# Making the block inverses of a two-direction scan once for two steps, by halves and in place

## The chip, the core and the metric

The kernel runs on one NeuronCore of a Trainium2 chip, in float32 throughout. The metric is the device time of one execution in microseconds (us). Of three runs of the kernel before, the median is 1346.3 us (1344.57 to 1348.67).

## The reference, cut to what matters

One layer of a hybrid diffusion backbone over 1024 latent tokens and 256 context tokens, width 1024: modulation, a combined input projection with a short convolution, a token mixer, an output projection, and a mixture of 16 experts. The change lies in the token mixer, which has a gated DeltaNet group (4 heads of 128) and a Mamba-2 SSD group (8 heads of 64), each run in both directions, context first:

```
decay = exp(G[i] - G[j]) for i >= j              # G: cumulated log gates of a chunk
L     = strict_lower((beta k) k^T * decay)
u, w  = solve(L + I, [beta v, beta k exp(G)])     # unit triangular
v_new = u - w S
o     = (q exp(G)) S + (q k^T * decay) v_new
S     = S exp(g_last) + k_tail^T v_new

# SSD group, per chunk
y_off  = C h * exp(a)
y_diag = (C B^T * exp(a[i] - a[j])) (x * dt)
h      = h exp(a_last) + B^T (x * dt * exp(a_last - a))
```

## The kernel before

The sequence is cut into ten chunks of 128 tokens (two of context, eight of latents). The scan is a list of twenty steps, `steps[s] = (s % 2, s // 2)`: direction d = 0 and d = 1 take turns, so that an even step is a chunk of the forward direction and the odd one after it a chunk of the backward direction. Steps 0 to 3 are context (only states), steps 4 to 19 are latent (states and outputs). No planner orders the work: each engine has its own loop over `s`, written out by hand, and semaphores tie the loops together. Within an iteration `s` an engine does things for `own` (step s), `nxt` (s + 1), `two` (s + 2) and `three` (s + 3).

TensorE (`pe_scan`), in the order of one iteration: `from_k` (key by state, L429), `block_w(nxt)`, `from_state` (L511), `solve` (L429), `block_vy(nxt)`, `from_chunk` (L522), `outputs` (L495, L496), `block_vp(nxt)`, `to_s` (L429), `to_state` (L532), `block_vq(nxt)`. Every float32 matmul here is two instructions in the trace. L448 is the one line of the four `block_` functions.

The triangular inverse of a 128-token chunk is made from the inverses of its four 32 x 32 diagonal blocks, which an earlier stage has left in DRAM (`xy_dram`) as X and as its transpose Y. `block_w` multiplies the off-diagonal part AT (key products times decays) by the diagonal inverses, and three more products (`vy`, `vp`, `vq`) put the blocks together. Between them ScalarE copies the products W and Q out of PSUM (`evac`, L601), and VectorE makes Y of them (`block_p`, L658, and `block_y`, L664). All of it is done for the next step during this one, with matmuls of 64 to 128 columns.

VectorE also masks the decays that a DMA has broadcast (`mask_dn`, 512 wide, and `mask_ssm`, 1024 wide, both L633), multiplies AT by them (`block_a`, L653), and does `rest` (L669), `scores` (L715), `y_off` (L699), `y_diag` (L706), `new_s` (L679) and `new_hs` (L691). ScalarE takes exponentials in place (`decay`, L565, `decay8`, L577), scales the keys (`tail_k`, L595) and the SSD input by the step size (`scaled_x`, L586), and copies U and the outputs. GpSimd does `query_e` (L770), `with_eg` (L754, L756), `decayed_hs` (L764) and `tail_x` (L777).

SyncE (SP) issues every load and store of the scan from one queue, in the order of `sp_scan`: for each step s three transfers of key products (`load_at(two)`, L834), four of the diagonal inverses (`load_xy(two)`, L844; both X and Y, written into one buffer for each direction), then `load_kg(two)` (L851), `load_e(three)` (L822), `load_e8(two)` (L859), `load_qk(two)` (L866), `load_kt(two)` (L872), and last `scan_store(own)` (L918), which waits until the outputs of this step are complete:

```
sp_.wait_ge(sem("s_o"), turn(d, nl(step) + 1))
sp_.wait_ge(sem("s_yd"), turn(d, nl(step) + 1))
```

`load_e8(two)` waits for `from_chunk` of this step, since that frees the buffer.

Ahead of the scan, `gates_second` on ScalarE (L2108 to L2110) takes three exponentials of gate columns, for which VectorE waits before `wtail` (L2363).

Of the kernel before, what the change touches and what calls it, by code (L numbers as in the profile page):

```python
# [5 lines left out]
P = 128  # L6
F32 = mybir.dt.float32
U32 = mybir.dt.uint32
ALU = mybir.AluOpType
# [6 lines left out]
def hybrid_block(nc, x, c, ctx, c_ctx, ada_w, ada_b, norm_g, w_in, conv_w, conv_b, dn_A_log, dn_dt_bias,  # L16
# [47 lines left out]
    with ExitStack() as es:  # L64
# [37 lines left out]
        eps1, eps_q = sb("eps1", [P, 1]), sb("eps_q", [P, 1])  # L102
# [213 lines left out]
        E, AT, Xd, Yd, W, Y, Q, kgT, qgT, QE, ktail, R, U, S = ([] for _ in range(14))  # L316
        E8, xdt, xw, hs, ost, XY = ([] for _ in range(6))
        for d in range(2):
            for lst in (W, Y, Q, kgT, qgT):
                lst.append(take(L4).rearrange("p (h n) -> p h n", h=DN_H))  # L320
            if d == 1:
# [6 lines left out]
                for dd in range(2):  # L328
                    XY.append(take(2 * L4).rearrange("p (x n) -> p x n", n=P))
                    Xd.append(XY[dd][:, 0:DN_H, :])  # L330
                    Yd.append(XY[dd][:, DN_H:2 * DN_H, :])
            for lst in (QE, ktail, R, U, S):
                lst.append(take(L4).rearrange("p (h n) -> p h n", h=DN_H))
            E8.append(take(SSM_H * P).rearrange("p (h n) -> p h n", h=SSM_H))
            for lst in (xdt, xw, hs):
# [14 lines left out]
        HI, TOP = slice(P // 2, P), slice(0, P - BL)  # L350
        A_R = ((TOP, slice(BL, P)), (slice(0, P), TOP))
        W_R = ((slice(0, P), slice(0, P)), (TOP, slice(BL, P)))
        Q_R = ((TOP, HI), (TOP, slice(0, P // 2)))
        Y_R = ((slice(0, P // 2), HI), (HI, slice(0, P // 2)))
# [54 lines left out]

        def hold(bank, n):  # L410
# [5 lines left out]
        def pe_first(pe):  # L416
            pe.wait_ge(sem("pfree"), NM - 1)
            pe.wait_ge(sem("s_at"), 1)
            pe.wait_ge(sem("ld_xy0"), 64)
            for h in range(DN_H):  # L420
                last = nc.tensor.matmul(bA[0][:, cols(h)], AT[0][:, h, :], Xd[0][:, h, :], start=True, stop=True)
            last.then_inc(sem("s_blk"), 1)

        def pe_scan(pe):
# [19 lines left out]
            def in_region(d, rc, lhsT, rhs, k=slice(0, P)):  # L444

                rows, cc = rc
                for h in range(DN_H):
                    last = mm(heads(bA[d][:])[rows, h, cc], lhsT[k, h, rows], rhs[k, h, cc], start=True, stop=True)  # L448
                return last

            def block_w(step):
                d, n = step
                pe.wait_ge(sem("s_at"), turn(d, n + 1))
                pe.wait_ge(sem(f"ld_xy{d}"), 64 * (n + 1))
                if n > 0:
                    pe.wait_ge(sem("s_py"), part(2, (d, n - 1), 2))
                in_region(d, W_R[d], AT[d], Xd[d]).then_inc(sem("s_blk"), 1)

            def block_vy(step):
                d, n = step  # L460
# [2060 lines left out]
```

## Time and profile before

| | |
|---|---|
| median of three runs | 1346.3 us (1344.57 to 1348.67) |
| the profiled execution: its time | 1342.35 us |
| its span, first to last instruction | 1340.6 us |
| TensorE busy | 1228.4 us, 92% |
| VectorE, ScalarE, GpSimd busy | 768.7, 429.4, 226.2 us |
| the scan | from about 550 us to about 756 us of the span |

The span is cut by the profiler into instructions with a start and a busy time. Matmuls are pipelined: the busy time of a group ends later than the next group begins, so the cost of a group on TensorE is read from its start to the start of the next one. An idle time in square brackets stands behind the instruction that ended it, with what released it.

### The profile page before, as it was taken

The numbers are of one execution on the slowest core, as the hardware profiler recorded it, in microseconds if no ns is written. First come the engines' busy times: TensorE is split into PE (matmuls) and PEld (weight loads), VectorE is DVE, ScalarE is ACT, GpSimd is POOL, SyncE is SP. The second block draws the span as 40 slices with busy tenths as digits, with TensorE's granted clock in tenths as the row PEclk, the third lists the DMA queues.
The fourth block names the chain that finished last, engine by engine and source line by source line (L and its number), as shares of the span: only waits on it lengthen the run. The fifth ranks groups of instructions, "written<-read, shape, count | busy, mean of one in ns | idle before, by whom it ended". The sixth has DMA issues, their size and how long they took to land.

```text
span 1340.6 us, 14739 instructions
## 1 busy us (share of the span) xinstructions
PE 1228.4 (92%) x5500; PEld 711.8 (53%) x5500; DVE 768.7 (57%) x1113; ACT 429.4 (32%) x1109; POOL 226.2 (17%) x205
## 2 busy tenths in 40 slices
PE   4999999999998999899999989981799999999992
PEld 3555555555544555588999744440444444444440
DVE  5299889887926778579898656647300101010116
ACT  5333232313111112567887545531101011010123
POOL 0300000020000021165677100001100101010112
PEclk9999999999998999999999999995799999999996
DMA  9923455442142443376766755526599999999967
GB/s 366 287 79 102 124 162 150 142 146 94 48 128 77 90 94 85 80 205 199 223 211 207 265 203 188 188 79 227 199 346 339 332 341 324 349 320 353 319 221 184
DMA packets 206164, 270.69 MB, mean 202 GB/s; under 512 B 73685, under 2 KB 122830, under 8 KB 206094
## 3 DMA queue, kind: packets, MB, share of 16 engines
q1 hardware_dynamic: 186182, 212.54, 48.2%
q0 software_dynamic: 13840, 50.86, 12.4%
q10 hardware_dynamic: 6072, 6.35, 1.4%
q8 instruction: 44, 0.72, 0.2%
q14 instruction: 26, 0.21, 0.1%
HBM read 217.75 MB, written 51.97 MB: 201 GB/s over the span
## 4 chain that ended last, share of the span: by engine, by line
PE 73%; DVE 13%; DMA 8%; SPq 2%; ACT 2%; issue 1%; POOLq 0%; DVEq 0%; ACTq 0%
PE ps L2045 18%; PE ps L1210 17%; PE ps L1233 8%; PE ps L1165 7%; PE ps L448 4%; PE ps L429 4%; DVE arena L2412 3%; DMA tok_dram<-arena 2%; DVE arena L2483 2%; DVE arena L2481 2%; DMA arena<-w_in 2%; DMA arena<-ada_w 1%; PE ps L522 1%; PE ps L1944 1%; PE ps L495 1%
## 5 line engine op out<-in xcount | busy, mean ns | idle before, releaser
L2045 PE MATMUL ps<-arena 128*128 128x512 f32 (+1 forms) x1072 | 424.9, 554 | 5.3 <-DMA arena<-w_in 5.3
L2045 PEld LDWEIGHTS ps<-arena 128*128 128x128 f32 x1072 | 201.6, 191 | 205.9 <-issue 195.4
L1210 PE MATMUL ps<-arena 128*128 128x512 f32 x512 | 226.8, 596 | 1.4 <-ACT arena L1359 1.4
L2412 DVE SCALAR_TENSOR_TENSOR arena<-arena,taps 128x1024 f32<-128x1024 f32 x160 | 207.5, 1297 | 5.5
L1210 PEld LDWEIGHTS ps<-arena 128*128 128x128 f32 x512 | 96.5, 191 | 116.6 <-issue 114.8
L1560 DVE TENSOR_TENSOR arena<-arena,ps 128x512 f32<-128x512 f32 x16 | 11.0, 688 | 223.3 <-PE ps L1210 223.3
L1165 PE MATMUL ps<-arena 128*128 128x512 f32 x256 | 115.5, 597 | 2.9 <-DMA arena<-w_out 2.9
L1233 PE MATMUL ps<-arena 128*128 128x512 f32 x256 | 112.5, 592 | 0.0
L448 PE MATMUL ps<-arena 128*128 128x128 f32 (+5 forms) x632 | 69.6, 253 | 7.6 <-DVE arena L658 3.9
L1233 PEld LDWEIGHTS ps<-arena 128*128 128x128 f32 x256 | 47.5, 190 | 54.0 <-issue 54.0
L1165 PEld LDWEIGHTS ps<-arena 128*128 128x128 f32 x256 | 46.5, 190 | 53.4 <-issue 49.5
L1377 ACT ACTIVATE arena<-ps 128x512 f32<-128x512 f32 x16 | 9.6, 598 | 198.7 <-PE ps L1210 198.7
L1642 POOL DMA_INDIRECT y_dram<-arena x14 | 22.3, 1594 | 289.5 <-DVE arena L1567 289.5
L448 PEld LDWEIGHTS ps<-arena 128*128 128x128 f32 (+4 forms) x632 | 62.4, 168 | 15.3 <-issue 8.7
L2227 ACT ACTIVATE arena<-arena,vcols 128x1280 f32<-128x1280 f32 (+1 forms) x20 | 25.9, 1297 | 137.0 <-DVE arena L2412 136.8
L1359 ACT ACTIVATE arena<-ps 128x512 f32<-128x512 f32 x32 | 19.0, 594 | 143.4 <-PE ps L1199 143.4
L1566 DVE TENSOR_SCALAR arena<-ps,arena 128x512 f32<-128x512 f32 x14 | 10.5, 750 | 91.7 <-PE ps L1233 91.7
L429 PE MATMUL ps<-arena 128*128 128x128 f32 x448 | 62.4, 282 | 0.2 <-DVE arena L669 0.2
L2428 DVE SCALAR_TENSOR_TENSOR arena<-arena,silu_c 128x256 f32<-128x256 f32 x112 | 57.0, 509 | 4.0
L1850 POOL DMA_DIRECT2D arena<-ada_w x16 | 14.4, 902 | 259.3 <-DVE arena L2428 217.9
L429 PEld LDWEIGHTS ps<-arena 128*128 128x128 f32 x448 | 55.3, 191 | 3.5 <-issue 1.5
L633 DVE TENSOR_TENSOR arena<-arena,neg_mask 128x512 f32<-128x512 f32 (+1 forms) x36 | 47.4, 1318 | 2.8 <-DMA arena<-g_dram 2.7
(336 smaller groups left out, 1579.2 us busy)
## 6 DMA issues: line engine op xcount, KB each, us to landing
arena<-exp_w_gate SPq DMA_DIRECT2D x16, 2048.0 KB, 11.1
arena<-exp_w_up SPq DMA_DIRECT2D x16, 2048.0 KB, 9.5
arena<-exp_w_down SPq DMA_DIRECT2D x16, 2048.0 KB, 10.8
arena<-ada_w POOLq DMA_DIRECT2D x16, 1024.0 KB, 6.4
arena<-w_in SPq DMA_DIRECT2D x28, 512.0 KB, 4.8
arena<-ada_w SPq DMA_DIRECT2D x4, 2048.0 KB, 19.6
arena<-x SPq DMA_DIRECT2D x16, 512.0 KB, 6.4
arena<-g_dram SPq DMA_DIRECT2D x16, 512.0 KB, 5.7
```

What stands on the lines that cost most here:

```text
L429: last = mm(out[:, h * P:(h + 1) * P], lhsT[:, h, :], rhs[:, h, :], start=True, stop=True)
L448: last = mm(heads(bA[d][:])[rows, h, cc], lhsT[k, h, rows], rhs[k, h, cc], start=True, stop=True)
L633: return nc.vector.tensor_tensor(out, out, bh(neg_mask[:, d, :], n), ALU.add)
L1165: last = mm(ps[2 + 2 * s + h][:], mixT[s][:, k, :], wo[:, k, h * 512:(h + 1) * 512], start=(k == 0), stop=(k == KD - 1))
L1210: last = mm(ps[gu_bank[s] + j][:], xsT[s][:, k, :], ew[s][j][:, k, :], start=(k == 0), stop=(k == KD - 1))
L1233: last = mm(ps[down_bank(e) + h][:], hidT[s][:, k, :], ew[s][2][:, k, h * 512:(h + 1) * 512], start=(k == 0), stop=(k == KF - 1))
L2045: last = mm(ps[3 * (m % 2) + gi][:, 0:w], wring[(m + 1) % NW][:, k, :], hT[:, k, o:o + w], start=(k == 0), stop=(k == KD - 1))
L2227: ins = a(dst, cacc[n_conv(mm) % 2][:, 0:w], ACT.Silu, bias=bcol)
L2412: ins = v.scalar_tensor_tensor(accg, cin_l[ci % 2][:, j // 3:j // 3 + GR, j % 3:j % 3 + GW], tp[:, j:j + 1], accg, ALU.mult, ALU.add)
L2428: ins = v.scalar_tensor_tensor(out, blk[:, k, :], silu_c[:, k, 0:1], out, ALU.mult, ALU.add)
L2481: link(v.tensor_tensor(tm, yo4[:, :, j, j + 1:BL].unsqueeze(3).to_broadcast([P, 3, n, j]), z4[:, :, j, 0:j].unsqueeze(2).to_broadcast([P, ...
L2483: link(v.tensor_tensor(z4[:, :, j + 1:BL, 0:j], z4[:, :, j + 1:BL, 0:j], tm, ALU.subtract))
```

## The change

- **Blocks for two steps at once, by halves.** In odd iterations only, the inverses of both directions of the next pair n are made: `block_near` (32 x 32 products of neighbouring blocks), `block_pairs`, `block_far` (64 x 64), `block_halves`. ScalarE takes all four out of PSUM (`near_out`, `pairs_out`, `far_out`, `halves_out`) and writes the results, negated, straight into the X and Y that the DMA has brought. W, Q, the four older block functions, `block_p` and `block_y` are gone. For a pair there are 16, then 16 and 8, then 8, then 8 matmuls.
- **Loads.** `load_at` for steps s + 2 and s + 3 and `load_xy` for the same two are issued together in even iterations; d = 1 gets two XY buffers in turn. `load_at` waits for `block_far` of the pair before.
- **Decays one step further ahead.** `load_e` and `mask_dn` are for s + 4, `decay` for s + 3.
- **Step size in the exponent.** A logarithm of the step size is added to the bias of `decay8`, so `scaled_x` falls away and `from_chunk` takes x itself.
- **Order.** `from_chunk` comes behind `outputs` and `to_s`; `mask_ssm(nxt)` comes ahead of `scores(own)`; `y_diag` comes behind `new_s`.

```diff
+        PAIRS = (((0, 1), (2, 3)), ((1, 0), (3, 2)))
+        FROM, INTO = (half(0), half(1)), (half(1), half(0))
...
+        def near(n, ds):
+            for h in range(DN_H):
+                for k in range(2):
+                    for d in ds:
+                        a, b = PAIRS[d][k]
+                        last = nc.tensor.matmul(heads(bA[d][:])[quarter(b), h, 0:BL], AT[d][quarter(a), h, quarter(b)],
+                                                x_of(d, n)[quarter(a), h, quarter(a)], start=True, stop=True)
+            return last
...
+            def block_near(n):
+                pe.wait_ge(sem("s_at"), turn(1, n + 1))
+                for d in range(2):
+                    pe.wait_ge(sem(f"ld_xy{d}"), 64 * (n + 1))
+                near(n, (0, 1) if n > 0 else (1,)).then_inc(sem("s_blk"), 1)
...
+            def block_far(n):
+                pe.wait_ge(sem("s_wq"), phase(n, 2))
+                for h in range(DN_H):
+                    for d in range(2):
+                        last = mm(heads(bA[d][:])[INTO[d], h, HALF:P], AT[d][FROM[d], h, INTO[d]],
+                                  x_of(d, n)[FROM[d], h, FROM[d]], start=True, stop=True)
+                last.then_inc(sem("s_blk"), 1)
...
             for s in range(-1, 2 * NS):
                 own = steps[s] if s >= 0 else None
-                nxt = steps[s + 1] if s + 1 < 2 * NS else None
+                n = pair_of(s)
                 if own and own[1] > 0:
                     from_k(own)
-                if own and nxt:
-                    block_w(nxt)
+                if n is not None:
+                    block_near(n)
                 if lat(own):
                     from_state(own)
                 if own:
                     solve(own)
-                if nxt:
-                    block_vy(nxt)
+                if n is not None:
+                    block_pairs(n)
+                if lat(own):
+                    outputs(own)
+                if own and own[1] < LAST:
+                    to_s(own)
+                if n is not None:
+                    block_far(n)
                 if lat(own):
                     from_chunk(own)
-                    outputs(own)
-                if nxt:
-                    block_vp(nxt)
                 if own and own[1] < LAST:
-                    to_s(own)
                     to_state(own)
-                if nxt:
-                    block_vq(nxt)
+                if n is not None:
+                    block_halves(n)
...
+            def pairs_out(n):
+                act.wait_ge(sem("s_blk"), phase(n, 2))
+                for d in range(2):
+                    a_, b = PAIRS[d][d]
+                    minus(x_of(d, n)[quarter(b), :, quarter(a_)], heads(bA[d][:])[quarter(b), :, BL:2 * BL])
+                    for a_, b in PAIRS[d]:
+                        last = minus(y_of(d, n)[quarter(a_), :, quarter(b)], heads(bA[d][:])[quarter(a_), :, 0:BL])
+                last.then_inc(sem("s_wq"), 1)
...
                 if own and own[1] > 0:
                     rest(own)
-                if lat(own):
-                    scores(own)
-                if own and two:
-                    mask_dn(dve, two)
-                if lat(own):
-                    y_off(own)
-                if nxt:
-                    block_p(nxt)
                 if lat(nxt):
                     mask_ssm(nxt)
                 if lat(own):
-                    y_diag(own)
-                if two:
+                    scores(own)
+                    y_off(own)
+                if s % 2 == 0 and two:
                     block_a(two)
+                    block_a(three)
+                if four:
+                    mask_dn(dve, four)
                 if own and own[1] < LAST:
                     new_s(own)
+                if lat(own):
+                    y_diag(own)
+                if own and own[1] < LAST:
                     new_hs(own)
-                if nxt:
-                    block_y(nxt)
...
-                    sp_.wait_ge(sem("s_blk"), part(4, (d, n - 1), 1))
+                    sp_.wait_ge(sem("s_blk"), phase(n - 1, 3))
...
-                if two:
+                four = steps[s + 4] if s + 4 < 2 * NS else None
+                if s % 2 == 0 and two:
                     load_at(two)
-                    load_xy(two)
+                    load_at(three)
+                if four:
+                    load_e(four)
                 if two and two[1] > 0:
                     load_kg(two)
-                if three:
-                    load_e(three)
+                if s % 2 == 0 and two:
+                    load_xy(three)
+                    load_xy(two)
                 if lat(two):
                     load_e8(two)
                     load_qk(two)
...
                 a(eGt[:], gb[:], ACT.Exp).then_inc(sem("g_act"), 1)
+                act.wait_ge(sem("g_act"), 6)
+                a(gb[:], sp[:], ACT.Ln, bias=tiny[:])
                 a(wtail[:], ga[:], ACT.Exp).then_inc(sem("g_act"), 1)
```

## Rows read from the trace of the kernel before

**Rows 1.** Busy time of each engine in one stretch of the latent steps, with granted clock

```profile
core 0: us, PE busy (x) PEld busy (x) DVE busy (x) ACT busy (x) POOL busy (x), PEclk, DMA share, GB/s
661.00:682.00 21.00, 21.00 (x224) 19.52 (x223) 18.73 (x29) 15.09 (x49) 15.33 (x11) 1.00 0.71 223
```

**Rows 2.** Timeline of TensorE, one even step: start us, busy us, instructions

```profile
665.91 1.06 PE L448 MATMUL ps<-arena 128*128 128x128 f32 x8
666.80 1.03 PE L511 MATMUL ps<-arena 128*128 128x256 f32 x4
...
668.56 1.06 PE L448 MATMUL ps<-arena 128*128 128x128 f32 x8
669.55 1.15 PE L522 MATMUL ps<-arena 128*64 128x64 f32 x32
670.63 0.49 PE L495 MATMUL ps<-arena 128*128 128x128 f32 x2
...
672.52 0.81 PE L448 MATMUL ps<-arena 128*96 128x64 f32 x8
673.17 1.11 PE L429 MATMUL ps<-arena 128*128 128x128 f32 x8
...
675.07 0.68 PE L448 MATMUL ps<-arena 96*64 96x64 f32 x8
675.68 1.16 PE L429 MATMUL ps<-arena 128*128 128x128 f32 x8
676.68 0.84 PE L448 MATMUL ps<-arena 128*96 128x96 f32 x8
```

**Rows 3.** Timeline of the DMA-issuing queue of SyncE in the scan

```profile
655.32 0.32 SPq L918 DMA_DIRECT2D scan_dram<-arena  x1
655.68 2.62 SPq L834 DMA_DIRECT2D arena<-kk_dram  x3
658.34 2.08 SPq L844 DMA_DIRECT2D arena<-xy_dram  x4
660.47 0.45 SPq L851 DMA_DIRECT2D arena<-eg_dram  x1
...
661.44 0.42 SPq L859 DMA_DIRECT2D arena<-g_dram  x1
...
679.16 3.36 SPq L844 DMA_DIRECT2D arena<-xy_dram  x4
```

**Rows 4.** Line L834: one issue, all 60 (ns min/median/max)

```profile
L834 SPq DMA_DIRECT2D arena<-kk_dram x60: 550/599/1597, 522.5 to 731.7; - x60
```

**Rows 5.** Line L844, issue to landing

```profile
DMA to landing us min/median/max: 1.7/2.0/4.0
```

**Rows 6.** Line L859, issue to landing

```profile
DMA to landing us min/median/max: 3.9/5.7/6.8
```

**Rows 7.** Groups by line and shape, 640 to 740 us

```profile
L577 ACT ACTIVATE arena<-arena,ga 128x128 f32<-128x128 f32 x80 | 24.3, 389 | 0.0
L633 DVE TENSOR_TENSOR arena<-arena,neg_mask 128x1024 f32<-128x1024 f32 x9 | 14.9, 1651 | 0.0
L715 DVE TENSOR_TENSOR arena<-arena 128x512 f32<-128x512 f32 x18 | 12.6, 743 | 0.0
L601 ACT ACTIVATE arena<-ps 96x256 f32<-96x256 f32 x10 | 3.7, 374 | 5.4 <-PE ps L448 5.4
```

**Rows 8.** Timeline of TensorE: start of the scan, steps 2, 4 and 18, end

```profile
553.38 1.13 PE L448 MATMUL ps<-arena 128*128 128x128 f32 x8 [1.93 <-ACT arena L601]
...
574.15 1.13 PE L429 MATMUL ps<-arena 128*128 128x128 f32 x8 [0.19 <-DVE arena L669]
...
591.01 1.13 PE L429 MATMUL ps<-arena 128*128 128x128 f32 x8
...
742.34 1.05 PE L429 MATMUL ps<-arena 128*128 128x128 f32 x8
...
755.61 0.39 PE L496 MATMUL ps<-arena 128*128 128x128 f32 x2
```

**Rows 9.** Timeline of ScalarE and VectorE around the gates

```profile
103.66 1.28 ACT L2227 ACT_TABLE_LOAD   x1
...
120.78 1.36 ACT L2227 ACTIVATE arena<-arena,vcols 128x1280 f32<-128x1280 f32 x1 [5.96 <-DVE arena L2412]
...
103.67 0.33 DVE L2363 TENSOR_TENSOR wtail<-wtail,sp 128x160 f32<-128x160 f32 x1 [1.05 <-ACT wtail L2110]
```

More of the change, by code:

```diff
@@ L408, in d_reader, with pair_of @@
             return {"yoff": "s_yoff", "ydiag": "s_yd"}[use2], turn(d, n - NC + 1)
+        def pair_of(s):
+            n = (s + 1) // 2
+            return n if s % 2 == 1 and n < NS else None
         def hold(bank, n):
@@ L627, in act_scan @@
                     a(ost[d][:, 0:QK], bC[d][:], ACT.Copy).then_inc(sem("s_o"), 1)
-                if nxt and nxt[1] < LAST:
+                if nxt and nxt[1] < LAST and s >= 0:
                     tail_k(nxt)
+                if n is not None:
+                    far_out(n)
+                    if lat(nxt):
+                        decay8(nxt)
+                    halves_out(n)
+                if s == -1:
+                    tail_k(nxt)
+                    decay(act, three)
         def masked(out, d, n):
@@ L721, in dve_scan @@
                 two = steps[s + 2] if s + 2 < 2 * NS else None
+                three = steps[s + 3] if s + 3 < 2 * NS else None
+                four = steps[s + 4] if s + 4 < 2 * NS else None
                 if own and own[1] > 0:
                     rest(own)
-                if lat(own):
-                    scores(own)
-                if own and two:
-                    mask_dn(dve, two)
-                if lat(own):
-                    y_off(own)
-                if nxt:
-                    block_p(nxt)
                 if lat(nxt):
@@ L887, in sp_scan @@
             sp_.wait_ge(sem("w_used"), NM + 1)
+            for step in steps[0:2]:
+                load_kt(step)
             sp_.wait_ge(sem("aux_used"), N_AUX)
             sp_.wait_ge(sem("ztok_out"), 16 * DI // P)
-            for s in range(-2, 2 * NS):
-                own = steps[s] if s >= 0 else None
+            for step in steps[2:4]:
+                load_e(step)
+            for s in range(0, 2 * NS):
+                own = steps[s]
                 two = steps[s + 2] if s + 2 < 2 * NS else None
                 three = steps[s + 3] if s + 3 < 2 * NS else None
-                if s < 0:
-                    load_kt(two)
-                    if s == -1:
-                        load_e(three)
-                    continue
-                if two:
+                four = steps[s + 4] if s + 4 < 2 * NS else None
+                if s % 2 == 0 and two:
                     load_at(two)
-                    load_xy(two)
+                    load_at(three)
+                if four:
+                    load_e(four)
                 if two and two[1] > 0:
                     load_kg(two)
-                if three:
-                    load_e(three)
+                if s % 2 == 0 and two:
+                    load_xy(three)
+                    load_xy(two)
                 if lat(two):
```

185 lines of the change are left out of this document (97 added, 88 removed).

## The prediction

> **What bounds the kernel now.** I first read the busy time by stretches. In the latent steps TensorE is busy 21.00 of 21.00 us at a granted clock of 1.00 (2.4 GHz), VectorE 18.73, ScalarE 15.09 [rows 1]. So the scan is bound by TensorE's own work, and what the change takes off TensorE counts, as far as nothing else is then late. Next the timeline of TensorE, for the price of each piece, from start to start [rows 2]. An even step lasts 676.68 - 665.91 = 10.77 us. Of it the block work (L448) is 0.89 + 0.99 + 0.65 + 0.61 = 3.14 us; in the odd step the first piece is narrower (busy 0.84 where the wide one shows 1.06), so about 0.67 and 2.92 in all. A pair of steps holds 6.06 us of block work. Of the rest I take from the same rows: `from_state` and `solve` 0.88 each (1.76 together), `from_chunk` 1.08, `outputs` 1.89, `to_s` and `to_state` 0.95 each, `from_k` 1.00: 7.63 a step. Third, the SyncE queue [rows 3, 4], since it issues every load in one order. Last, four times at which the scan stands: `solve` of step 2 at 574.15, of step 4 at 591.01, of step 18 at 742.34, the end at about 755.8 [rows 8]. Steps 4 to 18 are seven pairs in 151.3 us, 21.6 us a pair.
>
> **TensorE work, less.** A pair now has 56 small matmuls, two instructions each: 32 (near) + 48 (pairs) + 16 (far) + 16 (halves) = 112. No row shows 32 x 32 matmuls with four places of the array taking turns. The nearest is `from_chunk`: 32 instructions of 64 x 64 whose halves alternate, in 1.08 us, 0.034 us each. Upper bound: the 64-column block product, whose matmuls all go to one place, 8 in 0.61 us, 0.076 each [rows 2]. Lower bound: half the narrowest price, 0.017, as the matmuls have half the columns. I take 0.034: near 1.1, pairs 1.6, far 0.55, halves 0.55, 3.8 us, and 0.4 for more changes of shape (the first `outputs` group is busy 0.49 behind such a change [rows 2], which I read as 0.1 each). So TensorE has 4.2 us where it had 6.06, 1.9 less a pair; bound by TensorE alone a pair is 2 x 7.63 + 4.2 = 19.5 us.
>
> The row gives 0.034 us for an instruction. The Trainium skill ("TensorE: Matmul & The Clock Gate", Wait — 56ns, not 53.3ns?) has starts of matmuls never closer than about 25 ns, however small; by that estimate the 112 would be 2.8 us and not 3.8, and no lower than that.
>
> **ScalarE and VectorE, less.** `scaled_x` (eight copies) is gone. The new copies: twelve of 32 to 128 partitions. A 256-column one is 0.374 busy [rows 7]; back to back I take 0.28, and 0.18 for 128 columns: `near_out` 0.45, `pairs_out` (six) 1.2, `far_out` 0.65, `halves_out` 0.65, some 3 us a pair. Both engines have room [rows 1]. `block_p` and `block_y` leave VectorE. These gains are off the path.
>
> **SyncE: the loads come in one lump.** Here the gain goes. In an even iteration the queue issues two `load_at`, `load_e`, `load_kg`, two `load_xy`, and only then `load_e8`. Prices: three AT issues 3 x 0.6 plus gaps, 1.9 to 2.66, I take 2.05; four XY 2.13, at times 3.4 [rows 3, 4]; kg and e together 0.97 (660.47 to 661.44). Sum: 4.1 + 1.0 + 4.25 = 9.35 us, and 0.7 for an occasional long issue as at 679.16. The lump begins only when `scan_store` of the odd step before has been issued, which waits for `y_diag`. Call that moment 0. The last XY issue ends at 10.05 and lands 2.0 after its start [rows 5]: 11.5. `block_near` waits for both directions' XY, and behind it on TensorE stand `from_state`, `solve`, `outputs`, everything of the odd step. Without that wait TensorE would be there at about 9.7: `y_diag`, the store and its waits leave it some 1.2 us ahead, and the even step is 7.63 plus `to_state`, `block_halves` and the next `from_k`, less that lead. So the wait is about 2 us, and then: near 1.1, `from_state` 0.9, `solve` 0.9, pairs 1.6, `outputs` 1.9, `to_s` 0.95, far 0.55, `from_chunk` 1.1: 20.5. `y_diag` 0.7 and the store 0.5 close the loop at 21.7.
>
> There is a second way round the loop. `load_e8` for the next step is issued at 10.05 and lands in 3.9 to 5.7 [rows 6]; behind a drained queue I take 4.4. `mask_ssm` now stands ahead of `scores` on VectorE, so `scores`, `y_off`, `mask_dn`, `new_s` and `y_diag` wait for it: 14.4 + 1.2 to 1.65 + two `scores` at 0.65 to 1.2 each [rows 7] = 17 to 18.5, in time for `from_chunk` at 19.4 but late enough that `y_off`, `mask_dn`, `new_s`, `y_diag` (0.6 + 0.6 to 1.7 + 1.1 + 0.6) can end at 22. I put the pair at 22.1 us, + 0.5 on before, seven times: + 3.5.
>
> **Context steps.** These have slack on TensorE, so latency counts. `load_at` for the second pair now waits for `block_far` of the first. First near product out at 553.4 as before [rows 8]; pairs 1.6, `pairs_out` 1.2, far 0.55: 556.8; the lump 9.35 and the landing 1.5: 567.6; near, `solve`, pairs, `pairs_out`, `tail_k` (1.2), `far_out`, halves, `halves_out` (7.9): `solve` of step 2 at about 576 instead of 574.15. The same loop again, with `decay8` (eight exponentials of which each takes 0.3 back to back, 2.4) ahead of `halves_out`: `solve` of step 4 at about 594.2 instead of 591.0. + 3.2; it could be 0 to + 6.
>
> **The end.** Steps 18 and 19 lose the blocks of step 19, 2.9 us, but wait 0.6 for U before `outputs`: - 2.3.
>
> **The gates.** One logarithm and two table loads (1.28 each [rows 9]) come ahead of `wtail`, about 3 us for which VectorE waits (it waits 1.05 now). I cost it at nothing: TensorE is busy through that stretch, ScalarE has an idle 5.96 us before its next silu, and VectorE's convolution lags catch up in later waits. With that cover gone it is 3 us.
>
> **Sum.** + 3.5 + 3.2 - 2.3 = + 4.4, rounded up for waits of VectorE and GpSimd beside each other, to + 5. Against the profiled 1342.35 (span 1340.6 and 1.75 around it) that is 1347.4; against the median of 1346.3, which lies 3.95 above the profiled execution, 1351.3. What 0.3% means: 4 us, about what a measurement can tell here.
>
> **Rivals.**
> - *The lump is hidden, the scan stays bound by TensorE.* For it: TensorE is full now, and if small matmuls cost 0.025 (halfway between my price and its lower bound) and no issue is long, XY lands at 10.8 and the chain is 0.9 shorter. Against it: 9.35 us of issue are needed even so. Pair 20.4 us: 7 x (-1.2) + 1 - 2.3 = - 10, 1336. It decides from where the lump is shorter than about 8.5 us or begins before the store. Chance 0.27.
> - *Level.* The two come out even: pair 21.4, context + 2: 1345 to 1349. Chance 0.23.
> - *`load_e8` and the masks take over.* Landing 5.7, masks and scores slowed by GpSimd as in the mean row: pair 23.5, + 13 on the seven, 1360. Chance 0.13.
> - *The tiles don't overlap.* At 0.055 to 0.076 an instruction, 96 of them on the loop are 2 to 4 us more a pair, nine times: 1369 to 1387. For it: the one-place row. Against it: `from_chunk` at 0.034. Chance 0.07. The Trainium skill ("TensorEngine Tiling (Array Packing)", Gotcha 1: PSUM Pressure) says that different row tiles can't access one PSUM bank at the same time; here two row tiles of one direction do share a bank, while the other direction has another. No row of this trace has two row tiles in one bank.
> - *My forecast*, the lump sets the pair at 21.8 to 22.6: 1349 to 1356, chance 0.30.
>
> **From these, the numbers.** Slower by over 0.3% are the last rival, the one before it and nearly all of my own case: 0.47. Faster 0.28, within 0.3% 0.25. The range leaves out the tail beyond 1366 and a little below 1335. My own case alone: 1348 to 1357.
>
> **What would show it.** In the trace after: TensorE idle of 1 to 3 us before `block_near` in each odd latent step, released by the DMA of `xy_dram`; eight XY issues in a row on SyncE with `load_e8` some 10 us behind the store; VectorE idle before `mask_ssm` for `g_dram`; ScalarE's and VectorE's sums lower; near, pairs, far and halves at some 3.8 us a pair. I am wrong if `block_near` never waits (then the first rival), if a store is no longer what starts the lump, or if a pair of small products takes over 5 us.

## The result, and the profile after

The kernel after takes 1360.08 us (median of four runs, 1355.02 to 1360.67), the kernel before, beside it, 1345.43 us (four runs, 1342.49 to 1348.67). The ratio is 1.0116, with a 95% interval of 1.0089 to 1.0143: slower by 14.65 us, where + 5 was forecast. The profiled execution has a span of 1358.2 us.

Stretches of the profile after. The first answers to [rows 1]; the second is a long stretch of the latent steps, and the third the one where `block_near` has just been waited for.

```profile
core 0: us, PE busy (x) PEld busy (x) DVE busy (x) ACT busy (x) POOL busy (x), PEclk, DMA share, GB/s
661.00:682.00 21.00, 16.44 (x228) 14.16 (x224) 16.76 (x25) 12.43 (x40) 12.46 (x9) 0.92 0.66 175
608.00:740.00 132.00, 113.06 (x1532) 97.91 (x1532) 105.53 (x144) 85.51 (x269) 83.21 (x56) 0.94 0.64 195
678.00:681.60 3.60, 3.60 (x25) 3.10 (x12) 0.63 (x2) 1.60 (x6) 0.00 (x0) 0.53 0.94 200
```

TensorE was busy 21.00 of 21.00 us; now it is 16.44. Over 132 us it stands idle for 18.9, and its granted clock is 0.94 in the mean. All five engines are less busy in their shares, and the kernel is slower. No engine is full any more, so I look for the time in the waits.

SyncE's queue in one pair (answers to [rows 3]):

```profile
665.49 0.32 SPq L987 DMA_DIRECT2D scan_dram<-arena  x1
665.86 4.41 SPq L896 DMA_DIRECT2D arena<-kk_dram  x6
670.38 0.52 SPq L884 DMA_DIRECT2D arena<-g_dram  x1
670.95 0.42 SPq L917 DMA_DIRECT2D arena<-eg_dram  x1
671.42 4.69 SPq L910 DMA_DIRECT2D arena<-xy_dram  x8
676.16 0.45 SPq L925 DMA_DIRECT2D arena<-g_dram  x1
...
689.80 0.32 SPq L987 DMA_DIRECT2D scan_dram<-arena  x1
```

The lump is there: 10.3 us from the first key-product issue to `load_e8`, begun when the store of the odd step has gone out. The next such store comes 24.3 us later.

TensorE in the same pair (answers to [rows 2]):

```profile
677.65 0.45 PE L462 MATMUL ps<-arena 32*32 32x32 f32 x32 [2.06 <-DMA arena<-xy_dram]
678.03 2.04 PE L562 MATMUL ps<-arena 128*128 128x256 f32 x4
679.87 1.84 PE L475 MATMUL ps<-arena 128*128 128x128 f32 x8
681.64 0.42 PE L502 MATMUL ps<-arena 32*32 32x32 f32 x28
...
682.40 0.49 PE L546 MATMUL ps<-arena 128*128 128x128 f32 x2
...
686.55 1.15 PE L573 MATMUL ps<-arena 128*64 128x64 f32 x32 [0.59 <-DVE arena L778]
687.63 1.13 PE L583 MATMUL ps<-arena 128*128 128x256 f32 x4
688.69 0.68 PE L523 MATMUL ps<-arena 64*64 64x64 f32 x16
689.30 0.94 PE L475 MATMUL ps<-arena 128*128 128x128 f32 x6
```

`block_near` (L462) waits 2.06 us for the diagonal inverses, which land 11.8 us after the lump began. Then it takes 0.38 us to the next start, `block_pairs` 0.76, `block_halves` 0.61. But `from_state` and `solve` behind the wait take 1.84 and 1.77 from start to start instead of 0.88 each: in that stretch the granted clock is 0.53, near the level of 1.2 GHz. And `from_chunk` (L573) waits for `scores`.

VectorE in the same pair:

```profile
681.82 1.23 DVE L707 TENSOR_TENSOR arena<-arena,neg_mask 128x1024 f32<-128x1024 f32 x1 [3.19 <-DMA arena<-g_dram]
682.96 3.44 DVE L778 TENSOR_TENSOR arena<-arena 128x512 f32<-128x512 f32 x2
686.33 0.68 DVE L762 TENSOR_TENSOR arena<-ps,eG 128x512 f32<-128x512 f32 x1
686.93 1.17 DVE L707 TENSOR_TENSOR arena<-arena,neg_mask 128x512 f32<-128x512 f32 x1
688.02 1.11 DVE L742 SCALAR_TENSOR_TENSOR arena<-arena,eGt,ps 128x128 f32<-128x128 f32 x4
689.05 0.67 DVE L769 TENSOR_TENSOR arena<-arena,ps 128x512 f32<-128x512 f32 x1
```

`mask_ssm` (L707, 1024 wide) has waited 3.19 us for the transfer of `load_e8`. The two `scores` behind it (L778) take 3.44 us together, `y_diag` (L769) ends 23.9 us after the lump began, and the store follows at once.

The waits between 600 and 760 us (total, times, longest):

```profile
DVE arena L707 <- DMA arena<-g_dram: 17.1, 11, 3.2
...
PE ps L462 <- DMA arena<-xy_dram: 6.1, 4, 2.1
...
PE ps L573 <- DVE arena L778: 5.9, 7, 1.4
```

Last, times of the scan (answers to [rows 8]): `solve` and `to_s` of step 0, `solve` of step 4, `solve` and `from_chunk` of step 18, and the first matmul behind the scan.

```profile
561.09 2.08 PE L475 MATMUL ps<-arena 128*128 128x128 f32 x8 [0.87 <-ACT arena L642]
566.77 2.08 PE L475 MATMUL ps<-arena 128*128 128x128 f32 x8 [3.60 <-ACT arena L683]
...
596.92 1.13 PE L475 MATMUL ps<-arena 128*128 128x128 f32 x8 [0.46 <-DVE arena L732]
...
759.41 1.13 PE L475 MATMUL ps<-arena 128*128 128x128 f32 x8
...
765.37 1.15 PE L573 MATMUL ps<-arena 128*64 128x64 f32 x32 [2.10 <-DVE arena L778]
...
774.77 1.13 PE L448 MATMUL ps<-cum_mask,ident 128*128 128x256 f32 x4
```

Step 4 begins 5.9 us later than before. Steps 4 to 18 take 162.5 us instead of 151.3: 23.2 us a pair, + 11.2. From step 18 to the first matmul behind the scan it is 15.36 us, where before had 13.49 (to 755.83): + 1.9. Together + 19.0 in these two executions, whose spans differ by 17.6; the medians differ by 14.65. Of the 5.9 us, 1.8 are there long before the scan: the same silu of ScalarE starts at 512.56 us before (L2227) and at 514.36 after (L2298). From `solve` of step 0 to that of step 2 it is 18.7 us instead of 16.1, from there to step 4 17.1 instead of 16.9.

The line with 3.60 us is U of step 0: `to_s` of step 0 waits for the copy (L683), and ScalarE does that copy late. ScalarE's timeline there:

```profile
561.07 1.28 ACT L638 ACTIVATE arena<-arena,wtail 128x128 f32<-128x128 f32 x4
562.36 1.28 ACT L618 ACT_TABLE_LOAD   x1
563.66 2.44 ACT L618 ACTIVATE arena<-arena,ga 128x128 f32<-128x128 f32 x8
566.12 0.60 ACT L683 ACTIVATE arena<-ps 128x512 f32<-128x512 f32 x1
```

### The profile page after: what moved, and what is told of

Read it like the earlier page. It is cut to its first block, busy times and chain, and to the rows that moved or that the text cites. A ratio compares the mean times of both kernels' runs of the same rounds, so it can differ in the third digit from the quotient of the medians.

```text
span 1358.2 us, 15605 instructions
## 1 busy us (share of the span) xinstructions
PE 1212.7 (89%) x5980; PEld 686.2 (51%) x5980; DVE 759.7 (56%) x1073; ACT 421.0 (31%) x1064; POOL 228.4 (17%) x205
## 4 chain that ended last, share of the span: by engine, by line
PE 57%; DVE 16%; DMA 12%; SPq 6%; issue 5%; ACT 4%; POOL 0%; POOLq 0%; DVEq 0%; ACTq 0%
PE ps L2114 18%; PE ps L1279 13%; PE ps L1234 7%; PE ps L1302 6%; DVE arena L2483 3%; DMA y_dram<-arena 2%; DMA tok_dram<-arena 2%; PE ps L475 2%; DVE arena L2554 2%; DVE arena L2552 2%; DMA arena<-w_in 2%; SPq L896 1%; DMA arena<-g_dram 1%; DMA arena<-ada_w 1%; PE ps L2013 1%
## 5 line engine op out<-in xcount | busy, mean ns | idle before, releaser
L2114 PEld LDWEIGHTS ps<-arena 128*128 128x128 f32 x1072 | 201.7, 191 | 206.0 <-issue 195.4
L1279 PEld LDWEIGHTS ps<-arena 128*128 128x128 f32 x512 | 95.9, 190 | 115.7 <-issue 113.8
L475 PE MATMUL ps<-arena 128*128 128x128 f32 x448 | 68.8, 302 | 9.5 <-ACT arena L683 4.8
L1302 PEld LDWEIGHTS ps<-arena 128*128 128x128 f32 x256 | 47.5, 190 | 54.0 <-issue 54.0
L1234 PEld LDWEIGHTS ps<-arena 128*128 128x128 f32 x256 | 46.5, 190 | 51.6 <-issue 49.5
L475 PEld LDWEIGHTS ps<-arena 128*128 128x128 f32 x448 | 61.9, 211 | 17.8 <-issue 6.9
L2298 ACT ACTIVATE arena<-arena,vcols 128x1280 f32<-128x1280 f32 (+1 forms) x20 | 25.9, 1297 | 142.2 <-DVE arena L2483 142.0
L707 DVE TENSOR_TENSOR arena<-arena,neg_mask 128x512 f32<-128x512 f32 (+1 forms) x36 | 40.1, 1116 | 36.7 <-DMA arena<-g_dram 36.6
L847 POOL TENSOR_TENSOR arena<-arena,gates 128x1280 f32<-128x1280 f32 x4 | 9.8, 2450 | 212.9 <-DVE arena L2483 193.1
L778 DVE TENSOR_TENSOR arena<-arena 128x512 f32<-128x512 f32 x32 | 45.3, 1455 | 0.0
## 6 DMA issues: line engine op xcount, KB each, us to landing
arena<-ada_w SPq DMA_DIRECT2D x4, 2048.0 KB, 19.6
```

Of the source, the lines that this page charges most:

```text
L475: last = mm(out[:, h * P:(h + 1) * P], lhsT[:, h, :], rhs[:, h, :], start=True, stop=True)
L707: return nc.vector.tensor_tensor(out, out, bh(neg_mask[:, d, :], n), ALU.add)
L778: last = v.tensor_tensor(E8[d][:, hh, :], E8[d][:, hh, :], bh(BT[:, g, cols(t)], HPG), ALU.mult)
L1234: last = mm(ps[2 + 2 * s + h][:], mixT[s][:, k, :], wo[:, k, h * 512:(h + 1) * 512], start=(k == 0), stop=(k == KD - 1))
L1279: last = mm(ps[gu_bank[s] + j][:], xsT[s][:, k, :], ew[s][j][:, k, :], start=(k == 0), stop=(k == KD - 1))
L1302: last = mm(ps[down_bank(e) + h][:], hidT[s][:, k, :], ew[s][2][:, k, h * 512:(h + 1) * 512], start=(k == 0), stop=(k == KF - 1))
```

## The experiments

Twelve kernels. The table gives each ratio to the kernel before, and from the trace the mean pair (from `solve` of step 4 to that of step 18, by seven) and TensorE between 608 and 740 us. "Own work" is pair x busy / 132. Where a column is empty, those rows weren't needed. Each ratio is to the kernel before run beside that kernel; its medians lay between 1344.5 and 1345.4 us, and the interval of after reaches from 1.0089 to 1.0143, so store_late, mask_back and at_early overlap it, and what they save in time is likely, not certain.

| kernel | median us | ratio (95%) | pair us | PE busy of 132, clock | own work |
|---|---|---|---|---|---|
| before | 1345.43 | | 21.6 | 131.16, 1.00 | 21.5 |
| after | 1360.08 | 1.0116 (1.0089 to 1.0143) | 23.2 | 113.06, 0.94 | 19.9 |
| xy_early | 1350.75 | 1.0039 (1.0020 to 1.0057) | 22.4 | 110.05, 0.99 | 18.7 |
| store_late | 1354.37 | 1.0072 (1.0051 to 1.0093) | 22.9 | 111.25, 0.97 | 19.3 |
| mask_back | 1355.83 | 1.0084 (1.0057 to 1.0111) | 22.4 | 115.48, 0.96 | 19.6 |
| hold4 | 1361.75 | 1.0126 (1.0092 to 1.0161) | 23.2 | 116.50, 0.99 | 20.5 |
| xy_mask | 1350.18 | 1.0032 (1.0013 to 1.0051) | | 117.38, 0.95 | |
| xy_mask_at | 1347.98 | 1.0028 (1.0008 to 1.0048) | 21.9 | 115.12, 0.96 | 19.1 |
| at_early | 1355.57 | 1.0074 (1.0050 to 1.0098) | | 111.86, 0.97 | |
| before_exp | 1345.79 | 1.0010 (0.9991 to 1.0028) | | | |
| loads_odd | 1346.49 | 1.0007 (0.9989 to 1.0024) | 21.8 | 118.98, 0.95 | 19.6 |
| loads_odd_chunk | 1349.0 | 1.0021 (0.9998 to 1.0043) | | 111.47, 0.99 | |
| yd_early | 1349.66 | 1.0031 (1.0019 to 1.0044) | 22.1 | 114.52, 0.96 | 19.1 |
| yd_act | 1348.62 | 1.0028 (1.0014 to 1.0041) | 22.2 | 114.09, 0.96 | 19.1 |

The first four tell the suspected causes apart.

**xy_early: the lump without the XY loads of one direction.** Half of the eight XY issues go into the odd iteration, behind that store's own lump; the other half comes with the pair.

```diff
                 if s % 2 == 0 and two:
-                    load_xy(three)
+                    if s == 0:
+                        load_xy(three)
                     load_xy(two)
+                if s % 2 == 1 and four:
+                    load_xy(four)
```

> The changed kernel, with the diagonal inverses of the backward step loaded one iteration earlier (in the odd iteration before), so that the lump in an even iteration is four issues, about 2.1 to 2.6 us, shorter. Theory 1 (the lump of SyncE issues sets the loop, 24.3 us a pair measured): XY lands and the decays for the next step are issued 2 us sooner, the waits before block_near (up to 2.1 us) vanish, the clock stays at 1.00, and the pair shortens by 1.5 to 3 us: 10 to 20 us over the scan, back to about 1343 to 1350. Theory 2 (the loop is set by VectorE, whose scores take 3.4 us a pair of instructions beside GpSimd's work): less than 0.5 us a pair, 1356 to 1360.

It took 1350.75 us, some 9 us less than after, and the intervals are apart. The pair is 0.8 us shorter, less than the 1.5 to 3 of my first theory and more than the 0.5 of the second. Its waits between 600 and 760 us:

```profile
DVE arena L707 <- DMA arena<-g_dram: 15.4, 13, 2.1
...
PE ps L573 <- DVE arena L778: 10.5, 7, 2.1
...
PE ps L562 <- DVE arena L769: 9.7, 7, 1.5
```

No wait of L462 for `xy_dram` is left. What is left is VectorE: `from_chunk` waits for `scores` in every pair, `from_state` for `y_diag` in every pair. So the late XY is a cause, and the larger part of the loss went with it; taking it away uncovers the next wait.

**store_late: the lump begins earlier.** The store of the odd step is issued behind the XY loads instead of ahead of the key products.

```diff
-                if lat(own) and s < 2 * NS - 2:
+                if lat(own) and s < 2 * NS - 2 and (s % 2 == 0 or s + 1 == 2 * NS - 2):
                     scan_store(sp_, own)
...
                     load_xy(two)
+                if s % 2 == 0 and s > 0 and lat(steps[s - 1]) and s < 2 * NS - 2:
+                    scan_store(sp_, steps[s - 1])
```

> The changed kernel, with the store of an odd step's outputs issued behind the loads of the next even iteration instead of ahead of them. The lump then no longer waits for y_diag. Theory 1: the lump begins when load_kt of the odd step has been issued, some 1 to 3 us sooner, and the pair shortens by about as much: 1340 to 1352. Theory 2 (VectorE and GpSimd set the loop): no change beyond 3 us, 1356 to 1361.

1354.37 us: some 6 us less than after, between my two ranges. The start of the lump seems to matter, but its length stays, and `load_e8` still stands behind all of it (`mask_ssm` waits 3.1 to 3.2 us for `g_dram` in three places and 4.4 in one, where after has 3.2 at most).

**mask_back: `scores` doesn't wait for `load_e8`.**

```diff
-                if lat(nxt):
-                    mask_ssm(nxt)
                 if lat(own):
                     scores(own)
                     y_off(own)
+                if lat(nxt):
+                    mask_ssm(nxt)
```

> The changed kernel, with mask_ssm(nxt) on VectorE put back behind scores and y_off of the own step. Theory: a part of the loss is that scores waits for the decays of the next step (VectorE idle 17.1 us in 11 waits for g_dram) and then runs beside GpSimd, 3.44 us instead of 1.3. With the order turned, from_chunk no longer waits for scores and y_diag ends 1.5 to 3 us sooner in odd steps: 8 to 20 us faster than the changed kernel, 1340 to 1352. Rival: the wait for the inverses before block_near is what counts, and then this gives under 3 us.

1355.83 us, some 4 us less than after, where I expected 8 to 20. What the trace shows is clearer than the time. The group of `scores` between 600 and 740 us, first in after, then in mask_back:

```profile
L778 DVE TENSOR_TENSOR arena<-arena 128x512 f32<-128x512 f32 x24 | 33.7, 1444 | 0.0
```

```profile
L778 DVE TENSOR_TENSOR arena<-arena 128x512 f32<-128x512 f32 x24 | 17.0, 746 | 0.0
```

The same instruction takes half the time: in after it runs beside GpSimd's `query_e` and `with_eg` (682.52 to 685.85 in the pair shown), which wait for the transfer issued just behind `load_e8` and so start at the same time. Its saving is partly eaten by TensorE, which comes to `block_near` earlier and waits there longer; waits of mask_back:

```profile
DVE arena L727 <- DMA arena<-kk_dram: 13.0, 7, 3.0
...
PE ps L462 <- DMA arena<-xy_dram: 11.5, 6, 2.9
```

**hold4: the clock kept up.** Four 256-column matmuls into a bank that is free are put ahead of `block_near`'s waits.

```diff
             def block_near(n):
+                if n > 1:
+                    hold(bA[0], 4)
```

> The changed kernel, with four extra 256-column matmuls (0.43 us each, their results unused) ahead of the waits of block_near, n from 2 on. Theory (the granted clock, 0.87 to 0.94 in several stretches after and 1.00 before, costs time on the loop: from_state 1.84 and solve 1.77 us instead of 0.9 each after the idle time before block_near): TensorE is busy in that gap, the clock stays at 1.00, and each pair saves 0.5 to 1.5 us: 1346 to 1356. Rival: the slow matmuls lie in time that other waits would take anyway, and the extra ones delay block_near where it is not late: 1358 to 1366.

The clock was kept, and nothing was gained (1361.75 us, in the interval of after):

```profile
656.00:752.00 96.00, 84.39 (x1185) 72.78 (x1185) 78.14 (x105) 61.95 (x195) 59.70 (x41) 1.00 0.65 201
```

The rival in my expectation came out. Without the four matmuls (about 1.9 us a pair) TensorE's own work is 18.6 us, as in xy_early at 0.99. `from_state` and `solve` took 0.97 and 0.98 us there, and `from_chunk` waited 1.43 us for `scores` instead of 0.59. So the time at half clock lies where VectorE is waited for anyway. My theory that the clock is a cause by itself fell, with one reserve: in the pairs where XY is not late the four matmuls are work of their own, and a small gain by the clock could hide behind them.

**Combinations.** xy_mask is xy_early and mask_back together; xy_mask_at adds to it that the key products of the next pair are issued in the odd iteration, ahead of the store; at_early is after with that last edit alone.

```diff
-                if s % 2 == 0 and two:
+                if s == 0:
                     load_at(two)
                     load_at(three)
...
+                if s % 2 == 1 and three:
+                    load_at(three)
+                    load_at(four)
                 if lat(own) and s < 2 * NS - 2:
                     scan_store(sp_, own)
```

> Both edits together on the changed kernel: the backward inverses loaded one iteration earlier, and mask_ssm(nxt) behind scores and y_off. Alone they gave ratios of 1.0039 and 1.0084 to the kernel before, against 1.0116 for the changed kernel. Theory 1 (two loops of nearly equal length, one over the XY loads and one over mask and scores, so each edit alone is capped by the other): together they give more than the sum of 0.0077 + 0.0032, a ratio of 0.995 to 1.000, the pair at 20.5 to 21.3 us. Theory 2 (the loop is still SyncE's 9.4 us of issues before the decays of the SSD group): about the sum, 1.001.

> As xy_mask, and the six loads of key products for the next pair issued in the odd iteration ahead of the store (behind block_far, which frees their buffers), so that no lump waits for y_diag. If the lump is the cause of what is left, TensorE is again near full in the latent steps and the gain of the small matmuls shows: pair 20 us, ratio 0.990 to 0.997. If GpSimd (chain of query_e, with_eg, decayed_hs after the qk load) or VectorE is the bound by then, no gain over xy_mask.

> The changed kernel with only the key-product loads taken out of the even iteration and put ahead of the store of the odd one. Takes 4.4 of the 9.4 us of issues out of the stretch between the store and the XY landing. Theory 1: at least as good as xy_early, ratio 0.999 to 1.005; what is left is scores waiting for the mask. Theory 2 (only the landing of XY, not the lump as such): 1.004 to 1.008.

xy_mask took 1350.18 us, the same as xy_early, and missed both of my theories: what mask_back gave alone is not added. VectorE's `block_a` waits for the key products in it (13.7 us in 7 waits, up to 3.1), but it did so in mask_back too (13.0), so why nothing is added stays open. xy_mask_at took 1347.98 and at_early 1355.57 us, which is the second theory in both. at_early alone gives 4.5 us; on top of xy_mask the same edit gives 2 us, within both intervals.

Why at_early gives so little can be read from its queue. In one pair the key products are issued from 664.83 us on, `y_diag` ends at 664.88, and the store goes out only at 668.69, behind them. The first XY issue comes at 670.57, 5.7 us behind `y_diag`; in after it came 5.9 us behind the store (665.49, 671.42). `block_near` still waits for XY, 10.9 us in 6 waits. So in this pair the issues put ahead of the store did not move XY forward.

**before_exp: the step size in the exponent, alone in the kernel before.**

```diff
+                act.wait_ge(sem("g_act"), 6)
+                a(gb[:], sp[:], ACT.Ln, bias=tiny[:])
                 a(wtail[:], ga[:], ACT.Exp).then_inc(sem("g_act"), 1)
...
-                if lat(nxt):
-                    scaled_x(nxt)
```

> The kernel before with one part of the change alone: the step size added to the exponent's bias (a logarithm and two table loads ahead of wtail), and scaled_x, eight copies of 2.0 us a latent step on ScalarE, gone. ScalarE had room (15.09 of 21 us busy), and TensorE is the bound, so I expect the same, ratio 0.998 to 1.001. If the 3 us of table loads are not covered, 1.002; if ScalarE's queue was what delayed from_chunk (0.5 to 0.8 us idle before it in some steps), 0.995.

1.0010 (0.9991 to 1.0028): no effect that can be told; the interval goes up to 3.8 us, so by the time alone the 3 us of the table loads aren't ruled out. In the trace VectorE waits 4.27 us for `wtail` instead of 1.05 [rows 9] (in after as well), but the delay isn't passed on: the silu of ScalarE (L2227) that starts at 512.56 us in before starts at 512.29 in before_exp.

**loads_odd: the lump out of the even iteration.** mask_back, a second XY buffer for d = 0 as well, and from the third pair on all loads of the next pair in odd iterations: the XY where the even iteration had them, the key products ahead of the store.

```diff
-            return XY[0] if d == 0 else XY[1 + n % 2]
+            return XY[3 * (n % 2)] if d == 0 else XY[1 + n % 2]
...
+                if s % 2 == 1 and three:
+                    load_xy(three)
+                    load_xy(four)
...
+                if s % 2 == 1 and three:
+                    load_at(three)
+                    load_at(four)
                 if lat(own) and s < 2 * NS - 2:
                     scan_store(sp_, own)
```

> The changed kernel with mask_ssm behind y_off, two XY buffers for the forward direction too, and all loads of the next pair (XY of both directions, then the key products) issued in the odd iteration, XY behind block_near, the key products behind load_kt and ahead of the store. Even iterations issue 5 or 6 transfers, odd ones 19. xy_mask_at left block_near waiting 1.0 to 2.7 us (10 us in the latent steps) for the forward XY, and had the clock at 0.96. Theory 1 (that wait is what is left): block_near never waits, the clock stays at 1.00, pair 19.0 to 20.5 us, ratio 0.985 to 0.994. Theory 2 (GpSimd's chain from the qk load on, and TensorE's 0.69 us waits for U, are the bound by now): 1.000 to 1.003 as before.

1346.49 us, level with before (1.0007, 0.9989 to 1.0024), and some 14 us faster than after. In the medians that is the whole loss. In the trace it is the pairs that come back: steps 4 to 18 take 152.4 us, where after has 162.5 and before 151.3; step 4 still begins at 596.46. But TensorE isn't full again: my first theory (a ratio of 0.985 to 0.994) fell, and the result lies where the second had it (1.000 to 1.003). These are its waits, 600 to 760 us:

```profile
PE ps L563 <- DVE arena L770: 9.3, 7, 1.8
...
PE ps L547 <- ACT arena L684: 5.5, 8, 0.7
```

and TensorE and VectorE in one pair, as two fences:

```profile
670.21 0.45 PE L463 MATMUL ps<-arena 32*32 32x32 f32 x32
672.43 1.13 PE L563 MATMUL ps<-arena 128*128 128x256 f32 x4 [1.77 <-DVE arena L770]
```

```profile
666.12 3.17 DVE L728 TENSOR_TENSOR arena<-arena 96x384 f32<-96x384 f32 x2
669.85 0.90 DVE L708 TENSOR_TENSOR arena<-arena,neg_mask 128x512 f32<-128x512 f32 x1 [0.56 <-DMA arena<-g_dram]
670.67 1.11 DVE L743 SCALAR_TENSOR_TENSOR arena<-arena,eGt,ps 128x128 f32<-128x128 f32 x4
671.70 0.67 DVE L770 TENSOR_TENSOR arena<-arena,ps 128x512 f32<-128x512 f32 x1
```

`block_near` no longer waits for XY. `from_state` waits for `y_diag` (L770), in front of which VectorE has both `block_a` of the pair (L728, 3.17 us for two), a mask and `new_s`.

**Three tries at that wait.** loads_odd_chunk puts `from_chunk` ahead of `outputs` again. yd_early puts `y_diag` ahead of the second `block_a`. yd_act is yd_early with the first two `decay` of the scan behind the copy of U(0) on ScalarE. The core of each, in this order:

```diff
                 if lat(own):
+                    from_chunk(own)
                     outputs(own)
...
-                if lat(own):
-                    from_chunk(own)
```

```diff
                 if s % 2 == 0 and two:
                     block_a(two)
+                if lat(own):
+                    y_diag(own)
+                if s % 2 == 0 and two:
                     block_a(three)
```

```diff
+                if s == 0:
+                    decay(act, steps[2])
+                    decay(act, three)
...
                 if s == -1:
                     tail_k(nxt)
-                    decay(act, three)
```

> As loads_odd, and from_chunk back ahead of outputs on TensorE, as in the kernel before. In the order of the change TensorE waits 0.69 us for U in each even step, which from_chunk (1.08 us) used to cover. If that wait is on the path: 0.7 us a pair less than loads_odd or more, 5 to 8 us, 0.004 to 0.006 in the ratio. If scores are late by then, from_chunk waits instead and nothing is gained or some is lost.

> As loads_odd, and y_diag on VectorE ahead of the second block_a, mask_dn and new_s, instead of behind them. In loads_odd block_near no longer waited, but from_state did, 8.2 us in six odd steps (up to 1.9 each), for y_diag (which frees its PSUM bank), and VectorE was busy with two block_a of 1.6 us each beside GpSimd. If this wait, made by the changed order of y_diag, is what is left of the loss: 1.0 to 1.7 us less a pair, ratio 0.990 to 0.996. If only the clock (0.93 to 1.00) and the pace of GpSimd set the pair, 0.999 to 1.002.

> As yd_early, and the first two decays on ScalarE behind the copy of U of step 0. In the changed kernel TensorE sat idle 3.60 us before to_s of step 0, since that copy stood behind four key scalings, a table load and eight exponentials (5 us), and TensorE then ran at half its clock. If the start of the scan is a loss of its own: 1 to 3 us less than yd_early, 0.001 to 0.002 in the ratio. If the landing of the lump at about 568 us decides there anyway, nothing.

None gained. The waits of loads_odd_chunk (first fence) and of yd_early (second), 600 to 760 us:

```profile
PE ps L574 <- DVE arena L778: 16.9, 15, 1.7
```

```profile
DVE arena L770 <- PE ps L574: 33.1, 14, 4.5
...
PE ps L476 <- DVE arena L733: 14.4, 10, 2.3
```

In the first, TensorE waits for `scores` in every step. In the second, VectorE stands still for `from_chunk` (up to 4.5 us) with `new_s`, `new_hs` and `rest` queued behind `y_diag`, and TensorE then waits for `rest` (L733) ahead of `solve`. The wait moved each time, and yd_early (1.0031) came out above both of my ranges.

yd_act took away the 3.6 us for which `to_s` of step 0 waits for U: 0.69 us is left. But the scan gained little by it. `solve` of step 4 comes at 593.96 us instead of 596.73 in yd_early, yet 2.2 of these 2.8 us are there before the edit acts (the silu of ScalarE: 512.75 and 514.95). From `solve` of step 0 it is 18.2 us to that of step 2, where yd_early has 18.0, and 34.5 to that of step 4, where it has 35.1. The near products of the next pair wait for `block_a` now, which needs the decays that the edit put behind the copy:

```profile
566.98 0.65 PE L463 MATMUL ps<-arena 32*32 32x32 f32 x32 [1.01 <-DVE arena L730]
```

In the medians yd_act is 1 us below yd_early, within the intervals.

## Why the prediction was right, and where its size was off

The measured 1360 lies inside the range, but above my own case (1348 to 1357). It is inside because the range took in a rival as well. The mechanism held. The size was off, and all three terms of the sum erred the same way: together they gave + 4.4 us, where these two traces show + 19.0.

**Right: the direction and its mechanism.** Every sign that the prediction named is there: eight XY issues in a row, `load_e8` some 10 us behind the store (10.7), TensorE idle 2.06 us before `block_near` with the XY transfer as releaser (2 us forecast, landing at 11.8 where 11.5 was), `mask_ssm` waiting for `g_dram`, ScalarE's and VectorE's sums lower. That the lump costs the time is shown by experiments: half of the XY loads out of it gives 9 us; all of it out of the even iteration, with `mask_ssm` back (some 4 us alone), gives all the loss.

**Right: the gates.** Costed at nothing; before_exp shows nothing beyond its interval, and in its trace the longer wait is not passed on.

**Off: the seven pairs, + 11 where + 3.5 stood.** The term was the second way round the loop, `load_e8` to `y_diag`, put at 22 us and measured at 23.9 in the pair shown. Two pieces of it were mis-sized. The issue of `load_e8` came at 10.3 (10.05 forecast), but its transfer released `mask_ssm` 5.7 us later, not 4.4: "behind a drained queue I take 4.4" lay near the low end of [rows 6], where the median held. And "two `scores` at 0.65 to 1.2 each" took 1.72 each, 3.44 together against 2.4 at the upper end (the mean of 24 is 1.44). I had them near the mean row of 743 ns [rows 7], though the delay that holds them back also holds back GpSimd's work on the next transfer, so that both start together. mask_back shows the link: 746 ns again. The price of the rival named "`load_e8` and the masks take over", 23.5 us a pair and 1360, is what came out; I gave it 0.13.

**Not foreseen, but not the loss by itself:** `from_state` and `solve` at half clock behind the 2 us wait, + 1.8 us on the chain by way of TensorE. hold4 took it away and gained nothing, as the way by VectorE was as late in the pair shown.

**Off: the context, + 5.9 where + 3.2 stood.** Of the 5.9 us, 1.8 came before the scan, where kernels with the same code there differ by as much (514.95 and 512.75 us in yd_early and yd_act), so they need not be the change's. Another 1.3 lie between that silu and `solve` of step 0, 2.6 between steps 0 and 2, and 0.3 between 2 and 4. The prediction had about 1.9 by step 2 (576 against 574.15) and 1.3 more by step 4. It counted the queue of SyncE and not that of ScalarE, where the copy of U(0) stands behind `tail_k`, a table load and two decays, 5 us in all. That looked like the cause, but yd_act took that wait away and step 2 came no sooner behind step 0. Over the 18 us behind `solve` of step 0 TensorE is busy 15.6 us at a granted clock of 0.57 in yd_act (559 to 577 us), 12.3 us at 0.74 in yd_early (561 to 579), and 15.4 us at 1.00 in before (558 to 576). Whether the clock or the queues make these steps long stays open.

**Off: the end, + 1.9 where - 2.3 stood.** Steps 18 and 19 do lose block work. But `from_chunk` waits 2.10 us for `scores`, and the next step runs at a clock of 0.69 behind that (766 to 771.5 us). I counted the work that falls away and not the wait that it had covered.

**Off in the other direction: the small matmuls.** Forecast 3.8 us a pair and 0.4 for changes of shape, measured 0.38 (near), 0.76 (pairs) and 0.61 each for far and halves, 2.4 together. My lower bound of 0.017 us an instruction was undercut: 0.012 for near (0.38 / 32), 0.016 for the pairs (0.76 / 48); 0.034 was right only for those of 64 x 64 (0.61 / 16 = 0.038). The estimate of 2.8 from the Trainium skill ("TensorE: Matmul & The Clock Gate", Wait — 56ns, not 53.3ns?) was nearer than mine, but its floor of about 25 ns does not hold for these tiles in this trace: the measurement decides. The rival of 1369 to 1387 did not come. Of the rule of the Trainium skill ("TensorEngine Tiling (Array Packing)", Gotcha 1: PSUM Pressure) on row tiles in one PSUM bank this trace shows no cost: the near products, which share a bank in that way, are the cheapest of all.

**Where the gain went.** At a clock of 0.99 TensorE's own work is 18.7 us a pair (xy_early), 2.8 less than before. Even in loads_odd the pair is 21.8, of which 19.6 is own work, some at the lower clock (0.95 in the mean), and 2.1 idle: `y_diag` (9.3 us in 7 waits) and the copy of U (5.5 in 8), which `from_chunk` used to cover. The change has taken work from the engine that was full and put the order of the others on the path: `y_diag` behind two `block_a`, which the pairing puts into one step, and which take 1.62 us each in the median, where before they took 1.03. That these are what holds the last pair at 21.8 is argued from the waits. Two orders that took the one wait away brought another of the same size, so what a better order would be, and whether there is one below 21.6, stays open. No version that I ran is faster than the kernel before.

## What to carry to other kernels

When a change gathers the loads of two steps into one, add up the issue times on the queue before anything else: seven more issues ahead of `load_e8`, at 0.45 to 0.75 us each, are some 4.5 us, and the matmuls that they were to serve saved 2.8, and whatever is issued last in the lump (here the load for the masks) is late by its whole length. When a stall is forecast, ask which other engines it will release at the same moment, and price their work as running side by side, not by the mean row. When work is taken from a full engine, list what that work had covered; each of those waits is the next bound.

## What the runs showed of the hardware that I had not expected

- 32 float32 matmul instructions of 32 x 32 in four places of the array took 0.38 us from start to start (0.012 us each), 48 of them 0.76 us; row tiles of one direction share a PSUM bank and did not take turns visibly.
- Two 128 x 512 float32 products on VectorE, all operands in SBUF, took 1.28 us alone (mask_back, 674.24, GpSimd idle) and 3.44 us beside GpSimd's products of the same size (after, 682.96). The delay can fall on the other side: in xy_early the two took 1.28 us at 674.74 although `query_e` ran beside them, and `query_e` took 3.53 us where it took 1.65 in after:

```profile
673.61 3.53 POOL L832 TENSOR_TENSOR arena<-arena 128x512 f32<-128x512 f32 x1 [1.86 <-DMA arena<-qk_dram]
```

- Behind an idle 2.06 us TensorE ran at a granted clock of 0.53 for 3.6 us (`from_state` 1.84 us instead of 0.88); before the idle it had been at 1.00. With four matmuls put into the wait, which left 0.96 us of it idle, it stayed at 1.00. In loads_odd it stayed at 1.00 behind an idle 1.77 us at 672.43, but it was 0.62 (606.5 to 611 us) behind one of 1.78 us at 606.73, so the length of the idle time alone doesn't decide.
